# Differential attention: value products once per head, 512, 384, 256 and 128 columns wide, in place of one set of 128 columns per token tile

## What is computed

```python
def block(args):                       # one block of 128 queries
    qb, start = args
    q_chunk = (start + jnp.arange(Q_BLOCK)) // CHUNK        # CHUNK = 64
    mask = key_chunk[None, :] <= q_chunk[:, None]
    s = jnp.einsum('bqhcd,bkhcd->bhcqk', qb, k).astype(jnp.float32)
    p = jax.nn.softmax(jnp.where(mask, s, -jnp.inf), axis=-1)
    a = p[:, :, 0] - lam * p[:, :, 1]
    return jnp.einsum('bhqk,bkhe->bqhe', a.astype(v.dtype), v)
...
o = rms_norm(o, subln_g) * (1.0 - lam_init)
return o.reshape(B, S, H * DIFF_V_DIM) @ w_out
```

## Time and profile before

| | |
|---|---|
| median of 3 runs | 2516.66 us (2512.3 to 2519.39) |
| profiled execution, its own time | 2514.6 us |
| its span from the first to the last instruction | 2512.5 us |
| PE busy | 2353.4 us, 94% of the span |
| DVE busy | 1282.0 us, 51% |
| ACT busy | 778.0 us, 31% |
| mean granted clock of PE | 0.962 |
| differential attention, first scores to last head's copy | 1289.1 to 1366.8 us |

### The profile page before, as it was taken

How to read it: one execution, slowest core, us unless ns; L and a number is a source line. 1 busy time by engine, 2 the same in 40 slices (tenths; PEclk the granted TensorE clock), 3 DMA queues, 4 the chain that set the end, 5 groups by cost and what they waited for, 6 DMA issues and landing times.

```text
span 2512.5 us, 28641 instructions
## 1 busy us (share of the span) xinstructions
PE 2353.4 (94%) x11655; PEld 1887.7 (75%) x11659; DVE 1282.0 (51%) x1541; ACT 778.0 (31%) x1003; POOL 137.9 (5%) x92
## 2 busy tenths in 40 slices
PE   6999999996799999999987999999988678999998
PEld 5888888865688888787874788888767446788887
DVE  5434445637544345475467454445556764534443
ACT  3312233233333322353236322122333244322211
POOL 1000001102110100020000100000100000000000
PEclk9999999977899999999999999999999679999999
DMA  4333223210033232233320222332231200323231
GB/s 137 100 101 100 84 83 94 84 55 1 26 101 100 84 100 84 84 100 101 101 68 1 67 95 89 100 100 84 80 95 47 72 1 18 101 88 106 91 100 67
DMA packets 192321, 200.54 MB, mean 80 GB/s; under 512 B 6178, under 2 KB 187520, under 8 KB 192226
## 3 DMA queue, kind: packets, MB, share of 16 engines
q1 hardware_dynamic: 192226, 199.22, 25.1%
HBM read 191.93 MB, written 2.10 MB: 77 GB/s over the span
## 4 chain that ended last, share of the span: by engine, by line
PE 82%; DVE 11%; ACT 3%; issue 2%; DMA 1%; SPq 0%; POOL 0%; DVEq 0%; ACTq 0%
PE psum L548 81%; DVE w_lo L264 1%; DVE sm L1893 1%; PE psum L942 1%; DVE sm L1964 1%; ACT free_h L1100 1%; ACT w_hi L256 1%; PE psum L760 0%; DVE sq L1966 0%; DVE free_h L1473 0%; DVE h_lo L1469 0%; DVE rstd L1484 0%; DVE xg_lo L1466 0%; DVE free_h L1469 0%; DVE free_x L1466 0%
## 5 line engine op out<-in xcount | busy, mean ns | idle before, releaser
L548 PE MATMUL psum<-xg_lo,w_hi 128*128 128x512 f32 x1568 | 610.2, 392 | 5.0 <-DVE xg_lo L1466 2.7
L548 PE MATMUL psum<-xg_hi,w_hi 128*128 128x512 f32 x1520 | 596.3, 392 | 2.7 <-DVE w_lo L264 2.6
L548 PE MATMUL psum<-xg_hi,w_lo 128*128 128x512 f32 x1520 | 593.1, 390 | 0.0
L256 ACT ACTIVATE w_hi<-w_raw 128x2048 fp32r<-128x2048 f32 (+1 forms) x183 | 348.2, 1903 | 530.1 <-PE psum L548 515.2
L264 DVE TENSOR_TENSOR w_lo<-w_raw,w_hi 128x2048 fp32r<-128x2048 f32 (+1 forms) x183 | 419.1, 2290 | 177.3 <-ACT w_hi L256 177.2
L548 PE MATMUL psum<-h_hi,w_hi 128*128 128x512 f32 x1144 | 452.0, 395 | 4.5 <-DVE w_lo L264 2.7
L548 PE MATMUL psum<-h_hi,w_lo 128*128 128x512 f32 x1144 | 446.5, 390 | 0.0
L548 PE MATMUL psum<-h_lo,w_hi 128*128 128x512 f32 x1144 | 446.5, 390 | 0.0
L548 PEld LDWEIGHTS psum<-xg_lo,w_hi 128*128 128x128 f32 x1568 | 296.0, 189 | 68.5 <-issue 4.8
L548 PEld LDWEIGHTS psum<-xg_hi,w_hi 128*128 128x128 f32 x1520 | 286.8, 189 | 66.6 <-issue 5.7
L548 PEld LDWEIGHTS psum<-xg_hi,w_lo 128*128 128x128 f32 x1520 | 286.5, 188 | 59.9
(11 more groups left out here) (235 smaller groups left out, 2264.6 us busy)
## 6 DMA issues: line engine op xcount, KB each, us to landing
w_raw<-in_mlp_w SPq DMA_DIRECT2D x64, 1024.0 KB, 5.2
w_raw<-in_ffn_w_gate SPq DMA_DIRECT2D x22, 1024.0 KB, 5.3
w_raw<-in_ffn_w_up SPq DMA_DIRECT2D x22, 1024.0 KB, 5.3
w_raw<-in_ffn_w_down SPq DMA_DIRECT2D x16, 1024.0 KB, 5.0
w_raw<-in_diff_w_in SPq DMA_DIRECT2D x12, 1024.0 KB, 5.1
w_raw<-in_w_in SPq DMA_DIRECT2D x9, 1024.0 KB, 5.1
w_raw<-in_dsa_w_in SPq DMA_DIRECT2D x9, 1024.0 KB, 5.3
w_raw<-in_ffn_w_down SPq DMA_DIRECT2D x8, 768.0 KB, 4.3
```

The lines of the kernel that those rows point to most:

```text
L256: e.activation(w_hi[:, c % 2, 0:n], w_raw[:, c % 2, 0:n], ACT.Copy).then_inc(sem("hi_done"), 1)
L548: return pe.matmul(out, lhsT, rhs, start=start, stop=stop)
```

## The change

The differential attention keeps the transposed probabilities of a whole head. `ptc(u)` writes unit (g, n) into column block n of the tiles J = 0 to n of a set of four (free_x2[8..11] for even heads, [12..15] for odd ones). A new function `head_values(g)` then issues four matmuls for the head: for J = 0 the columns 0 to 511, for J = 1 those from 128, for J = 2 from 256 and for J = 3 from 384. It stands in PE's loop behind `transposes(u)` at u = 4(g+1)+1, and the last head's behind the loop. `values` is left to the sparse attention. ACT's `out_tile` moves by one unit, from u % 4 == 1 to u % 4 == 2, and `ptc` waits on `_pv` only at the first unit of a head, for the head two back.

```diff
+                def head_values(g):
+                    pe.wait_ge(*use(name, "_ptc", 4 * g + 4))
+                    if g >= 2:
+                        pe.wait_ge(*use(name, "_oc", g - 1))
+                    for J in range(NT):
+                        last = mm(bank[6 + g % 2][:, J * P:S], v2[:, J, g * P:(g + 1) * P],
+                                  free_x2[:, 8 + 4 * (g % 2) + J, J * P:S], J == 0, J == NT - 1)
+                    last.then_inc(use(name, "_pv")[0], 4)
...
                     transposes(u)
-                    if u >= 1:
+                    if dsa and u >= 1:
                         values(u - 1)
-                values(len(units) - 1)
+                    if not dsa and u % NT == 1 and u > NT:
+                        head_values(u // NT - 1)
+                if dsa:
+                    values(len(units) - 1)
+                else:
+                    head_values(KT - 1)
...
-                    if u >= 2:
+                    g, n = units[u]
+                    if dsa and u >= 2:
                         act.wait_ge(*use(name, "_pv", u - 1))
+                    if not dsa and g >= 2 and u % NT == 0:
+                        act.wait_ge(*use(name, "_pv", 4 * (g - 1)))
...
                     else:
-                        last = a(free_x2[:, 8 + 2 * (u % 2), 0:w], bank[4 + u % 2][:, 0:w], ACT.Copy)
+                        t0 = 8 + 4 * (g % 2)
+                        last = a(free_x2[:, t0:t0 + n + 1, n * P:(n + 1) * P],
+                                 bank[4 + u % 2][:, 0:w].rearrange("p (a q) -> p a q", q=P), ACT.Copy)
...
-                    if u % NT == 1 and u > NT:
+                    if u % NT == (1 if dsa else 2) and u > NT:
                         out_tile(u // NT - 1)
```

More of the change, by code:

```diff
@@ L957, in values @@
                     for J in range(n + 1):
[L958 to L963, removed]
+                        for cc in range(2):
+                            dst = bank[6 + u // NT % 2][HD * cc:HD * cc + HD, u % NT * P:(u % NT + 1) * P]
+                            v = v2[:, J, (2 * g + cc) * HD:(2 * g + cc + 1) * HD]
                             last = mm(dst, v, free_x2[:, 8 + 2 * (u % 2) + cc, J * P:(J + 1) * P], J == 0, J == n)
```

## The result

| | before | changed |
|---|---|---|
| median of 7 runs each | 2514.29 us (2512.3 to 2519.39) | 2527.15 us (2523.22 to 2530.55) |
| span of the profiled execution | 2512.5 us | 2522.1 us |
| mean granted clock of PE | 0.962 | 0.962 |

The ratio is 1.0041, with a 95% interval from 1.0028 to 1.0054: 7 to 13.6 us more, 10.3 in the middle; the two medians lie 12.9 us apart. So it is slower, clear of the scatter, though the low end of the interval is a little under the 7.5 us that the prediction took as the least a measurement can tell. The forecast was 2526 and +9.6. It started from a median of 2516.66 us for the kernel before, of three runs; with seven it is 2514.29.

The account below looks back on a forecast made before the run. A loop through PE, DVE and ACT was taken to pace the differential attention. 7.5 + 0.8 - 1.2 + 2.5 = +9.6 us gave 2524.2 for the profiled execution, 2526 us for the median, range 2515 to 2535.

Parts of the forecast that it names:

- The six heads: Products ahead of the scores of 4g+4, g = 1 to 6: 2.15 us replace 0.90, 6 x 1.25 = +7.5 us.
- Copy and square on ACT: Moved behind the exponentials of 4g+4: with a square 1.60 us, 0.28 over the slack, three times, +0.8 us.
- The first head: Unit 0's products leave their place; unit 4's scores start earlier but wait for banks exp(2) reads: -1.2 us.
- The end: After the last units, head 6's products and copy delay the last head's products and copy: +2.5 us (1.5 to 3).
- `ptc` in pieces: ACT's copy of transposed probabilities in pieces of 128 columns costs about the same as a plain copy: nothing taken.
- Rival 1: Wide passes cheaper than their columns say, eight in 1.15 us: +2.6 us, 2519 us, no change; chance 0.2.
- Rival 2: PE's clock falls in its longer idle gaps: 2548 us if in every head, 2537 in half; chance 0.13.

Follow-up runs that it names:

- the second experiment: Changed kernel with each head's four wide matmuls dealt out over three places, its ACT copy one head later: 2520.08 us, ratio 1.0009 against the kernel before.
- the execution without a fall of the clock: Changed kernel with extra identity transposes on PE in the gaps where it waits for DVE: 2532.22 us, ratio 1.0063 against the kernel before.
- the version that beat both kernels: Kernel before with its 128-column value products issued one unit later up to unit 28, at the old distance from unit 29: 2510.54 us, ratio 0.9974.

## Why the prediction was right, point by point

- **The six heads**, forecast 6 x 1.25 = 7.5: the full-clock head is 10.17 against 8.93, 6 x 1.24 = 7.4. Both halves of the step held: the products' own time, 2.15 us scaled from one 512-column pass (the 512-column product in the second experiment shows the same 1.02 us for two passes as the earlier trace rows), and that what is taken out elsewhere gives nothing back (ahead of the transposes of 4g+3 PE waits 0.98 us, 0.54 before, about 1.1 by the forecast).
- **Copy and square on ACT**, forecast 3 x 0.28 = 0.8: 3 x 0.34 = 1.0 (two of the three in heads, one behind the last maxima), gone when they are put back.
- **The first head**, forecast -1.2: from the first maxima to the second 9.70 us against 10.90. The scores of unit 4 did wait for ACT's exponentials, 0.32 us:

```profile
1298.11 2.08 PE L548 MATMUL psum<-arena,free_x 64*128 64x512 f32 x4 [0.32 <-ACT free_h L1111]
```

- **The end**, forecast +2.5: 6.62 - 4.22 = 2.4. The copy of head 6, 0.6 us in the forecast's chain, gave back 0.5 when it was moved behind `ptc(31)`.
- **`ptc` in pieces**: 0.49 us for 384 columns (1374.18 above) against 0.47 in the earlier trace rows. Nothing to speak of, as forecast.
- **Sum.** Forecast +9.6; the stage in the execution without a fall of the clock is +9.56. The changed kernel's stage is +12.0, the 2.4 more being the falls, which the sum doesn't hold.
- **Rival 1** (cheap wide passes) is out: the eight passes fill 2.25 us. The spacing of about 131 against 81 ns that the Trainium skill gives (TensorE: Matmul & The Clock Gate, Back-to-back issue gap) doesn't hold for these full 32-bit products: the traces have 0.43 us a pass against 0.113.
- **Rival 2** (the clock) had a chance of 0.13, and in a mild form it happened, next to the forecast mechanism and not in its place: two heads, 10.89 and 12.18 us in place of 10.16 and 10.51 where the clock held, 2.4 us of the stage. What it priced too high is a fall: 3.6 us a head in the prediction, 0.7 and 1.7 here. The comparison of gaps that spoke against it failed. I held single gaps of 1.1 us against a gap of 1.44 that the clock outlived in the earlier trace rows. In the changed kernel it fell twice with no gap above 0.98 us, after several waits close behind each other, and in the three heads from 1333.79 on, with the same waits, it did not fall. The Trainium skill (the section named in the prediction) has a clock that goes up and down with short pauses between groups of matmuls, and this trace agrees so far: two falls in the six heads. What decides whether a given head loses the clock stays open: neither the longest gap nor the busy share of a stretch does, since 1.86 of 3.0 us came ahead of a fall and 1.87 of 3.0 and 3.06 of 5.0 did not.

That the total still met the forecast, 2527 against 2526, is partly luck. The forecast stood on a median of before that was 2.4 us too high, and the clock's falls, which it left out, added about as much. From the better median, +9.6 would have been 2523.9, and the measured medians are 12.9 apart, not 9.6. The spans of the two profiled executions are just 9.6 us apart, but that has luck in it too: in the profiled execution the changed kernel leaves the stage 11.65 us late by the trace's clock and ends 9.6 us late. At the weights' next split on DVE (1404.55 before, 1415.63 after) it is 11.1 us late, near 1850 10.4, at the end 9.6, and from the stage's end on this is all code that the change doesn't touch.

## What to carry to other kernels

Before work is gathered into fewer, larger instructions, find the loop that sets the pace and ask where in it the gathered block will stand: a block costs its whole length there, while the pieces it replaces may have stood where the engine was waiting anyway. The idle time of the engine that waits last, ahead of one instruction per turn (0.81 us here), says that the slot ahead is on the loop, and it is also the most that can be won by moving work out of it: 0.55 us a head here, in the version that beat both kernels. And when PE's waits grow, read the granted clock turn by turn, and don't rely on a single longer gap elsewhere that the clock outlived: here it fell in some turns and not in others with the same waits.

## What the runs showed of the hardware

A full 32-bit product of 512 columns takes two passes of 0.43 us, one of 128 columns two of 0.113: its time goes nearly with its columns (3.8 times for 4), and wide products save only some 0.1 us on 1280 columns.

The clock fell twice in six heads with no wait of PE above 0.98 us, and stayed up in the three heads behind them with the same waits. A fall cost 0.7 and 1.7 us.

The same code in a stage differs from one execution to another by several microseconds, and with it the granted clock. Before (first two rows) and the wide products dealt out (last two), in the input products of the sparse attention, which no version touches:

```profile
1860.00:1892.00 32.00, 29.78 (x164) 21.23 (x162) 25.18 (x57) 15.53 (x23) 0.00 (x0) 1.00 0.21 66
1892.00:1935.00 43.00, 37.55 (x302) 30.68 (x300) 23.81 (x44) 14.63 (x23) 1.29 (x1) 1.00 0.18 46
```

```profile
1866.00:1900.00 34.00, 31.78 (x166) 22.60 (x164) 25.71 (x58) 16.10 (x23) 0.00 (x0) 0.95 0.20 63
1900.00:1945.00 45.00, 39.09 (x302) 31.70 (x300) 24.24 (x45) 14.60 (x23) 1.28 (x1) 0.96 0.18 47
```

The same work takes 32 and 43 us in the one and 34 and 45 in the other. The version with PE filled lost 5.3 us in the same place (its lateness against before went from 10.0 us at 1845 to 15.3 at 1949), which is why its gain in the attention doesn't show in its profiled execution's whole time; whether that holds for its other three runs can't be seen. It is also why a median that moves by 2 or 3 us says little here, and the stage's own rows say more, as long as the falls of the clock in them are counted.
